# Two attentions whose bias and mask are added by VectorE from tiles loaded in final order, in a one-core fp32 kernel of two transformer blocks

## The reference

```
logits[i,j] = scale * q_i . k_j + c_i - c_j,   c = cumsum over tokens of log_sigmoid(f_logit + b_f)
logits[i,j] = -inf where j > i;   p = softmax over j
```

```
logits[i,j] = scale * q_i . k_j + rel_bias[bucket(i - j), h],   -inf where j > i
```

## Time and profile before

| | |
|---|---|
| median of 3 runs | 2568.65 us (2568.54 to 2568.66) |
| profiled execution | 2565.43 us |
| its span in the trace | 2563.6 us |
| PE / DVE / ACT / POOL busy | 2529.5 / 2016.9 / 1303.7 / 52.6 us |

### The profile page before, as it was taken

How to read it: one execution, slowest core, us unless ns; L and a number is a source line. 1 busy time by engine, 2 the same in 40 slices (tenths; PEclk the granted TensorE clock), 3 DMA queues, 4 the chain that set the end, 5 groups by cost and what they waited for, 6 DMA issues and landing times. The chain is left out here.

```text
span 2563.6 us, 47253 instructions
## 1 busy us (share of the span) xinstructions
PE 2529.5 (99%) x14452; PEld 2190.5 (85%) x14452; DVE 2016.9 (79%) x3098; ACT 1303.7 (51%) x2041; POOL 52.6 (2%) x45
## 2 busy tenths in 40 slices
PE   8999999999999999999999999999999999999997
PEld 7888888888888888888888888878888888888886
DVE  7778775689887887887889775676888888888888
ACT  5444344565554454544555454454545546546456
POOL 0000000000000000000000014200000000000000
PEclk9999999999999999999999999999999999999999
DMA  7786874558888888888886644445455656556554
GB/s 278 265 279 199 279 261 155 187 185 265 279 282 280 279 285 281 279 282 279 281 280 202 197 165 133 131 154 184 155 186 171 204 177 190 195 172 205 188 164 157
DMA packets 160693, 562.01 MB, mean 219 GB/s; under 512 B 18132, under 2 KB 18429, under 8 KB 160637
## 3 DMA queue, kind: packets, MB, share of 16 engines
q1 hardware_dynamic: 132428, 459.04, 54.1%
q10 hardware_dynamic: 27792, 101.20, 12.2%
q0 software_dynamic: 416, 1.06, 0.2%
HBM read 559.12 MB, written 2.11 MB: 219 GB/s over the span
## 5 line engine op out<-in xcount | busy, mean ns | idle before, releaser
L300 PE MATMUL bank<-H,w_hi 128*128 128x512 f32 (+1 forms) x4480 | 1414.0, 394 | 11.9 <-DVE w_lo L1266 9.8
L1215 DVE TENSOR_TENSOR w_lo<-w_raw,w_hi 128x1024 fp32r<-128x1024 f32 x900 | 1092.6, 1223 | 142.0 <-ACT w_hi L730 136.6
L300 PEld LDWEIGHTS bank<-H,w_lo 128*128 128x128 f32 x4416 | 831.3, 188 | 190.3
L730 ACT ACTIVATE w_hi<-w_raw 128x1024 fp32r<-128x1024 f32 x900 | 912.5, 1051 | 11.6 <-PE bank L300 5.6
L300 PE MATMUL bank<-H,w_lo 128*128 128x256 f32 x4416 | 871.7, 278 | 0.0
L300 PEld LDWEIGHTS bank<-H,w_hi 128*128 128x128 f32 x4480 | 690.2, 189 | 18.5 <-issue 12.7
L300 PE MATMUL bank<-U,w_hi 128*128 128x512 f32 x1984 | 627.8, 396 | 2.4 <-DVE w_lo L1215 1.3
L751 ACT ACTIVATE scratch<-bank 128x256 f32<-128x256 f32 x356 | 136.6, 384 | 739.2 <-PE bank L300 739.0
L300 PEld LDWEIGHTS bank<-U,w_lo 128*128 128x128 f32 x1984 | 372.8, 188 | 86.3
L300 PE MATMUL bank<-U,w_lo 128*128 128x256 f32 x1984 | 401.7, 281 | 0.0
L300 PEld LDWEIGHTS bank<-U,w_hi 128*128 128x128 f32 x1984 | 308.1, 188 | 7.0 <-DVE w_lo L1215 3.5
(11 more groups left out here) (214 smaller groups left out, 1137.8 us busy)
## 6 DMA issues: line engine op xcount, KB each, us to landing
w_raw<-in_w_ff SPq DMA_DIRECT2D x256, 512.0 KB, 5.1
ada_w<-in_w_ada ACTq DMA_DIRECT2D x192, 512.0 KB, 4.6
w_raw<-in_w_up SPq DMA_DIRECT2D x176, 512.0 KB, 3.8
w_raw<-in_w_z SPq DMA_DIRECT2D x96, 512.0 KB, 4.8
w_raw<-in_w_in SPq DMA_DIRECT2D x88, 512.0 KB, 4.2
w_raw<-in_w_gate SPq DMA_DIRECT2D x64, 512.0 KB, 4.4
w_raw<-in_w_down SPq DMA_DIRECT2D x64, 384.0 KB, 3.1
w_raw<-in_w_down SPq DMA_DIRECT2D x64, 320.0 KB, 3.4
```

What stands on the lines that cost most here:

```text
L300: return nc.tensor.matmul(out, lhsT, rhs, start=start, stop=stop, skip_group_check=True)
L730: A(w_hi[:, slot, :], w_raw[:, slot, :], ACT.Copy).then_inc(sem("w_high"), 1)
L1215: TT(w_lo[:, slot, :], w_raw[:, slot, :], w_hi[:, slot, :].bitcast(F32), ALU.subtract)\
```

## The change

The added terms no longer go through PE. In the first attention, POOL stores the 8 rows -c_j to memory (`gate_rows`, 12 KB), loads each back as a tile of 128 equal rows (`key_bias[h % 2]`, 192 KB), and adds the mask to it. DVE adds this tile to the scores in one operation of 384 columns, writes the sum to `prob`, takes the maxima from there, and ACT exponentiates in place. In the second attention `relrow` is stored 128 times per head (8 x 128 rows of 1,536 bytes, 1.57 MB in place of 12 KB), so that a load with a step of one row less one element gives the rows in final order; DVE adds them in two operations. The matmuls with `decay_pick`, identity x `MASK_r` and `flip` go, with the small operations that prepared them (two roundings on ACT, some small copies on DVE). The constants shrink from 640 KB to 512 KB.

```
-IDENT_AT, LEOL_AT, SPARE_AT, MASK_AT, FLIP_AT, CONST_N = 0, 128, 512, 768, 1152, 1280
+IDENT_AT, LEOL_AT, GT_AT, MASK_AT, CONST_N = 0, 128, 512, 640, 1024
...
-        log_cols = scratch[:, 2944:3024].rearrange("p (b n) -> p b n", b=2)
-        decay_rows = rounded("decay_rows", [40, 384], "scratch", 2560)
-        decay_pick = rounded("decay_pick", [40, 8], "small", 440)
+        gate_rows = scratch[0:N_HEADS, 2560:2944]
+        key_bias = [scratch[:, 2560:2944], adaf[:, 768:1152]]
...
-            pe.wait_ge(sem("f.log_cols"), 2)
-            mm(bank[5][0:40, 0:128], log_cols[:, 0, :], LE, True, False)
-            mm(bank[5][0:40, 128:384], log_cols[:, 0, :], LEO, False, False)
-            mm(bank[5][0:40, 256:384], log_cols[:, 1, :], LE, False, True).then_inc(sem("f.summed"), 1)
+            pe.wait_ge(sem("f.logs"), 1)
+            logs = [small[:, 112 + 8 * b:120 + 8 * b] for b in range(2)]
+            mm(bank[5][0:8, 0:128], logs[0], LE, True, False)
+            mm(bank[5][0:8, 128:384], logs[0], LEO, False, False)
+            mm(bank[5][0:8, 256:384], logs[1], LE, False, True).then_inc(sem("f.summed"), 1)
...
-                        pe.wait_ge(sem(name + ".exps"), 2 * h - 2)
+                        pe.wait_ge(sem(name + ".biased"), h - 1)
                     q, k = tl.qs[h % 2], zb(k0 + k_step * h)
                     mm(s[:, 0:128], q[:, 0:128], k[:, 0:128], True, False)
-                    mm(s[:, 128:384], q[:, 128:256], k, False, False)
-                    mm(s[:, 0:384], decay_pick[:, h:h + 1].to_broadcast([40, P]), decay_rows[:, :], False, False)
-                    last = mm(s[:, 0:384], ident_r[:, :], MASK_r[:, :], False, True)
-                    last.then_inc(sem(name + ".scores"), 1)
+                    mm(s[:, 128:384], q[:, 128:256], k, False, True).then_inc(sem(name + ".scores"), 1)
...
-                    pe.wait_ge(sem("at2.exps"), 2 * h)
+                    pe.wait_ge(sem("at2.biased"), 2 * h)
                 q, k = at2.qs[h % 2], zb(36 + h % 2)
                 mm(bank[2][:, 0:128], q[:, 0:128], k[:, 0:128], True, False)
-                mm(bank[2][:, 128:384], q[:, 128:256], k, False, False)
-                pe.wait_ge(sem("relb_landed%d" % (h % 2)), 16 * (h // 2 + 1))
-                mm(bank[2][:, 0:128], flip, relb[h % 2][:, 128:256], False, False)
-                mm(bank[2][:, 128:384], flip, relb[h % 2], False, True).then_inc(sem("at2.scores"), 1)
+                mm(bank[2][:, 128:384], q[:, 128:256], k, False, True).then_inc(sem("at2.scores"), 1)
...
-            A(decay_rows[:, :], bank[5][0:40, 0:384], ACT.Copy).then_inc(sem("f.rows_high"), 1)
+            A(gate_rows, bank[5][0:8, 0:384], ACT.Copy, scale=-1.0).then_inc(sem("f.rows"), 1)
...
                 def exps(h):
                     act.wait_ge(sem(name + ".maxes"), 2 * h + 2)
-                    if h >= 2:
-                        act.wait_ge(sem(name + ".p_turned"), h - 1)
                     for b, (lo, up) in enumerate(((0, 128), (128, 384))):
                         c = 128 + 2 * h + b
-                        A(tl.prob[h % 2][:, lo:up], bank[2 + h % 2][:, lo:up], ACT.Exp, bias=small[:, c:c + 1],
+                        A(tl.prob[h % 2][:, lo:up], tl.prob[h % 2][:, lo:up], ACT.Exp, bias=small[:, c:c + 1],
                           accum_out=small[:, c + 16:c + 17]).then_inc(sem(name + ".exps"), 1)
...
                     dve.wait_ge(sem(name + ".scores"), h + 1)
+                    dve.wait_ge(sem(name + ".bias_ready"), h + 1)
+                    if h >= 2:
+                        dve.wait_ge(sem(name + ".p_turned"), h - 1)
+                    TT(tl.prob[h % 2], bank[2 + h % 2][:, 0:384], key_bias[h % 2], ALU.add).then_inc(sem(name + ".biased"), 1)
+                    dve.wait_ge(sem(name + ".biased"), h + 1)
                     for b, (lo, up) in enumerate(((0, 128), (128, 384))):
                         c = 128 + 2 * h + b
-                        v.tensor_reduce(small[:, c:c + 1], bank[2 + h % 2][:, lo:up], AX_X, ALU.max, negate=True)\
+                        v.tensor_reduce(small[:, c:c + 1], tl.prob[h % 2][:, lo:up], AX_X, ALU.max, negate=True)\
                             .then_inc(sem(name + ".maxes"), 1)
...
                 dve.wait_ge(sem("at2.scores"), h + 1)
+                dve.wait_ge(sem("relb_landed%d" % (h % 2)), 16 * (h // 2 + 1))
+                if h >= 2:
+                    dve.wait_ge(sem("at2.p_turned"), h - 1)
+                prob = at2.prob[h % 2]
+                TT(prob[:, 0:128], bank[2][:, 0:128], relb[h % 2][:, 128:256], ALU.add).then_inc(sem("at2.biased"), 1)
+                TT(prob[:, 128:384], bank[2][:, 128:384], relb[h % 2], ALU.add).then_inc(sem("at2.biased"), 1)
                 for b, (lo, up) in enumerate(((0, 128), (128, 384))):
                     c = 128 + 2 * h + b
-                    v.tensor_reduce(small[:, c:c + 1], bank[2][:, lo:up], AX_X, ALU.max, negate=True)\
+                    dve.wait_ge(sem("at2.biased"), 2 * h + b + 1)
+                    v.tensor_reduce(small[:, c:c + 1], prob[:, lo:up], AX_X, ALU.max, negate=True)\
...
+            def gate_row(h):
+                if h == 1:
+                    pool.wait_ge(sem("ada_acc"), 1 + ADA0["qk"] + 16)
+                if h >= 2:
+                    pool.wait_ge(sem("at1.biased"), h - 1)
+                row = bass.AP(t["gate_rows"].tensor, h * 384, [[0, P], [1, 384]])
+                pool.dma_start(key_bias[h % 2], row).then_inc(sem("gate_row_landed%d" % (h % 2)), 16)
+            def mask_row(h):
+                pool.wait_ge(sem("gate_row_landed%d" % (h % 2)), 16 * (h // 2 + 1))
+                nc.gpsimd.tensor_tensor(key_bias[h % 2], key_bias[h % 2], MASK, ALU.add).then_inc(sem("at1.bias_ready"), 1)
+            pool.wait_ge(sem("con_landed"), 32)
+            pool.wait_ge(sem("f.rows"), 1)
+            pool.dma_start(t["gate_rows"], gate_rows).then_inc(sem("gate_rows_stored"), 16)
+            pool.wait_ge(sem("gate_rows_stored"), 16)
+            for h in range(N_HEADS):
+                gate_row(h)
+                mask_row(h)
             pool.wait_ge(sem("relrow_ready"), 1)
-            pool.dma_start(t["rel_rows"], relrow[:, :]).then_inc(sem("relrow_stored"), 16)
+            copies = bass.AP(t["rel_rows"].tensor, 0, [[P * REL_W, N_HEADS], [REL_W, P], [1, REL_W]])
+            pool.dma_start(copies, relrow.unsqueeze(1).to_broadcast([N_HEADS, P, REL_W])).then_inc(sem("relrow_stored"), 16)
             pool.wait_ge(sem("relrow_stored"), 16)
             def bias_rows(h):
                 if h >= 2:
-                    pool.wait_ge(sem("at2.scores"), h - 1)
-                rows = bass.AP(t["rel_rows"].tensor, h * REL_W, [[1, P], [1, 256]])
+                    pool.wait_ge(sem("at2.biased"), 2 * h - 2)
+                rows = bass.AP(t["rel_rows"].tensor, h * P * REL_W + 127, [[REL_W - 1, P], [1, 256]])
                 pool.dma_start(relb[h % 2], rows).then_inc(sem("relb_landed%d" % (h % 2)), 16)
...
-    con = np.concatenate([ident, le, one, le, one, gt, causal, 0 * one, causal, ident[:, ::-1]], 1)
+    con = np.concatenate([ident, le, one, le, gt, causal, 0 * one, causal], 1)
...
-    t["rel_rows"] = nc.dram_tensor("rel_rows", (N_HEADS, REL_W), F32, kind="Internal").ap()
+    t["rel_rows"] = nc.dram_tensor("rel_rows", (N_HEADS, P, REL_W), F32, kind="Internal").ap()
+    t["gate_rows"] = nc.dram_tensor("gate_rows", (N_HEADS, 384), F32, kind="Internal").ap()
```

30 lines of the change are left out of this document (4 added, 26 removed).

## The result

The changed kernel takes 2576.61 us (median of 8 runs, 2576.08 to 2577.76), the kernel before 2568.56 us in the same comparison (8 runs, 2567.27 to 2568.66). The ratio is 1.0035, with a 95% interval of 1.0025 to 1.0045: slower by about 8 us, where 10 us less had been forecast. The profiled execution took 2576.55 us, its span 2574.5 us. Lines have moved: L300 is now L290, L441 L429, L1215 L1189, L730 L713, L751 L734, L866 L845, L559 L542.

What follows compares the result with a forecast made beforehand. PE, busy 99% of the span, was taken as the bound. Terms 6.2 + 5.2 + 0.3 - 0.6 - 0.8 - 0.25 = 10.05 us less than 2568.65 gave 2558.6 us, forecast range 2556.9 to 2561.3, 8-in-10 range 2556.5 to 2564.5.

Steps and rivals of the forecast that it cites:

- PE's saving, first attention: Removed matmuls between q.k and v's transposes save PE 0.78 us per head, 6.2 us over 8 heads.
- PE's saving, second attention: Without the flip matmuls, H's matmul follows q.k sooner: 0.65 us per head, 5.2 us over 8 heads.
- scores(1): First attention: DVE's addition delays exps(0) and so scale_q(1), and PE waits 0.6 us more.
- Heads 6 and 7: Second attention: v comes late for PE's transposes; losses of 0.8 us at head 6 and 0.25 at head 7.
- POOL's part at 0: First attention: POOL's gate-row loads and mask additions cost 0, tiles ready in time and SBUF conflicts covered by DVE's idle.
- 0.12 per product beside POOL: First attention: DVE's 384-column product took 0.665 us beside POOL, 0.12 above 0.55, one such loss per head covered.
- The start: Kernel start: 128 KB fewer constants ahead of weights that ACT waits for; gain 0 to 0.35 us, taken as 0.3.
- The big store, second block: At about 1407 us, the 1.57 MB store beside the weight stream costs 0, upper end 4.3 us.
- The prediction's own sign of being wrong: Near 1410 us: the prediction would be wrong if ACT waits for w_raw there.
- Rival 2: Second block: the store holds up the weights by 2 to 5 us, giving 2561 to 2564 us; chance 0.14.
- Rival 5: Second block: store time goes by rows, 230 us, so the first bias is late and the kernel takes 2665; chance 0.06.

Runs made afterwards that it cites:

- e3: The changed kernel with its 1,536 KB store issued in 16 pieces of 96 KB as the convolution units are computed; 2557.91 us, ratio 0.9966 to the kernel before.
- e11: e3 with head 0's gate row load and GpSimd mask addition about 165 us later; 2557.15 us, ratio 0.9958 to the kernel before.

## Why the prediction was wrong, point by point

- **PE's saving, first attention (6.2 us).** Right: 8 x 0.74 = 5.9. The 0.78 was mis-sized by 0.04.
- **PE's saving, second attention (5.2 us).** Right: about 0.66 a head.
- **`scores(1)` (0.6 lost).** Right: 1.01 - 0.44 = 0.57.
- **Heads 6 and 7.** Right in mechanism, a little too dear. From scores to transposes, against the transposes of the earlier trace rows and scores at 1677.68 and 1697.00:

```profile
1687.06 0.89 PE L290 MATMUL bank<-Z,G 128*128 128x128 f32 x4
1694.03 0.44 PE L542 MATMUL bank<-con,Z 128*128 128x128 f32 x2 [0.50 <-DVEq L1696]
1706.44 0.82 PE L290 MATMUL bank<-Z,G 128*128 128x128 f32 x4
1711.67 0.44 PE L542 MATMUL bank<-con,Z 128*128 128x128 f32 x2 [0.23 <-DVEq L1696]
```

  Head 6 takes 6.97 us as before, so it gives nothing (forecast: costs 0.15). Head 7 takes 5.23 instead of 5.77 and gives 0.54 (forecast: 0.4).
- **POOL's part at 0.** Wrong by 0.7 us (168.2 us from 198 us to the first scores instead of 167.4), and for a reason that the step did not look for. It asked whether POOL's tile comes in time, and it does: DVE never waits for POOL. It weighed the lock in the attention, where DVE has slack: splits do last 2.05 and 2.04 us instead of 1.22 there when an addition of POOL was running (387.39 and 394.65 us), against the forecast 1.22, and nobody waits for them. But head 0's addition runs at 208 us, some 160 us ahead of the attention, and there the 0.8 us by which it lengthens a DVE operation reach PE. By the Trainium skill's rule of the lock ("SBUF — State Buffer", "Who interferes with whom"), that a DVE instruction with two SBUF inputs contends with a GpSimd one that reads SBUF, the trace agrees (1.27 us instead of 0.48 beside an addition of 1.01); the prediction's 0.12 per product beside POOL was too mild a reading.
- **The start (0.3).** At 198 us PE is 0.2 us ahead (197.79 instead of 198.01).
- **The sum without the store.** 5.9 - 0.57 + 0.2 - 0.7 gives 4.8 for the first part, where 4.95 is measured at the store's issue; the second gives 9.3 - 4.95 = 4.35 by the spans of `e3` and before, forecast 4.15. Together 9.3 of 10.05.
- **The step that failed: "The big store, second block ... I cost it at 0, since weight loads there land in time in the trace, with 4.3 as the upper end".** It took the peak of all engines together, 367 GB/s, as the rate that a transfer of this form can reach, and the gap below it as free. 1.57 MB from 8 neighbouring partitions went at 1.57 MB / 34.6 us = 45 GB/s, with 8 packets of 642 ns in flight, which holds 8 engines for 27 us, and each weight piece needs those engines too. The cost was 18.3 us: 14.3 of idle PE, and 4 mostly of lower clock. The prediction's own sign of being wrong, that ACT waits for `w_raw` near 1410, came true with a wait of 13.44 us. Rival 2 named the mechanism and sized it by the same wrong rate. Rival 5 scaled the time by rows, which would have been 230 us, and looked only at the landing; the landing (about 1437 us) was over 100 us ahead of the first scores, and the time was lost in the weight stream meanwhile. The prediction had a row that was nearest in form, the 12 KB from the same 8 partitions in 1.8 us, or 7 GB/s, and used it for rival 5 alone. Between 7 and 367 GB/s the landing was unknown between 4.3 and 230 us, and that range belonged into the sum of the weight stream, not only into the landing.

## What to carry to other kernels

A transfer's size says little: ask over how many partitions and outer entries it runs, for how long it holds its engines, and what else uses them meanwhile. A few partitions as source of much data are worth a detour (a small store, then a copy within memory), or the transfer is cut into pieces that are issued as the work goes on. And an operation moved to an idle engine is charged where it runs: the lock between POOL and DVE cost nothing in the stage with slack and 0.7 us in the one without; run later, it cost nothing there either (`e11`).
